# A two-layer diffusion backbone: logits beside the turns, a reordered router, and the last norm on three engines

## The reference

```
logits = h @ w_router                              # 384 x 8
top_v, top_i = lax.top_k(logits, 2); top_p = softmax(top_v)
gates = sum(one_hot(top_i, 8) * top_p[..., None])
act = silu(einsum('bnd,edf->bnef', h, wg)) * einsum('bnd,edf->bnef', h, wu)
y = einsum('bnef,efd->bnd', act * gates[..., None], wd)      # f = 2816
x = layer_norm(ALPHA * x + gate * y, ln_gain, ln_bias)
```

## Time and profile before

| | before |
|---|---|
| median of 3 runs | 2077.76 us (2075.3 to 2078.76) |
| the profiled execution: time, span | 2079.98 us, 2078.2 us |
| instructions | 22944 |
| TensorE busy | 1790.9 us (86%) |
| VectorE, ScalarE, GpSimd busy | 600.3, 392.2, 55.7 us |
| granted TensorE clock, mean | 0.905 of full |
| read from memory | 397.48 MB |

### The profile page before, as it was taken

One profiled execution on the slowest core, in us unless ns is written; L12 is line 12 of the kernel. 1 busy time (PEld: TensorE's weight loads), 2 busy tenths in 40 slices (PEclk: granted clock), 3 DMA queues, 4 the chain that ended last, 5 costly groups with the idle time before them and its releaser, 6 DMA issues.

```text
span 2078.2 us, 22944 instructions
## 1 busy us (share of the span) xinstructions
PE 1790.9 (86%) x8823; PEld 1008.5 (49%) x8824; DVE 600.3 (29%) x1105; ACT 392.2 (19%) x788; POOL 55.7 (3%) x78
## 2 busy tenths in 40 slices
PE   4998888999987978878899986779997699999982
PEld 1764577888854845665234432223333244444320
DVE  1555564333334735653120010111001020000115
ACT  1333414222213323322010010010001010000100
POOL 1000000000000100001000000000000000000000
PEclk8897889999997988978999996679998799999996
DMA  9244414333342444143986669995565954443490
GB/s 327 82 151 146 162 65 156 121 122 122 122 142 102 161 137 161 61 183 134 374 322 240 228 236 389 395 388 192 198 219 190 390 195 144 152 145 125 154 367 38
DMA packets 198798, 401.95 MB, mean 193 GB/s; under 512 B 10872, under 2 KB 51832, under 8 KB 198688
## 3 DMA queue, kind: packets, MB, share of 16 engines
q1 hardware_dynamic: 195280, 389.06, 52.1%
q0 software_dynamic: 3408, 11.34, 1.6%
HBM read 397.48 MB, written 2.88 MB: 193 GB/s over the span
## 4 chain that ended last, share of the span: by engine, by line
PE 75%; DMA 8%; DVE 7%; SPq 4%; issue 3%; ACT 2%; POOL 0%; ACTq 0%; DVEq 0%
PE ps L1423 24%; PE ps L1722 15%; PE ps L1766 7%; PE ps L1727 5%; PE ps L1733 4%; PE ps L1682 3%; DMA d_ring<-in_w_moe_up 3%; SPq L520 3%; PE ps L1380 3%; PE ps L1773 2%; DMA gu_ring<-in_w_moe_up 2%; DMA qkv<-in_w_moe_up 2%; PE ps L1515 2%; PE ps L1779 2%; PE ps L1493 1%
## 5 line engine op out<-in xcount | busy, mean ns | idle before, releaser
L1340 DVE TENSOR_TENSOR cst<-cst,ps 128x256 f32<-128x256 f32 (+2 forms) x92 | 34.3, 373 | 826.9 <-ACT cst L862 826.9
L1423 PE MATMUL ps<-d_ring_parts,scratch_parts 128*128 128x512 f32 (+1 forms) x444 | 172.8, 389 | 10.1 <-issue 5.0
L1722 PE MATMUL ps<-gu_ring,hT 128*128 128x512 f32 x384 | 172.6, 594 | 0.0
L869 ACT ACTIVATE cst<-ps 128x256 f32<-128x256 f32 (+1 forms) x92 | 31.8, 346 | 586.5 <-PE ps L1749 586.5
L1423 PE MATMUL ps<-gu_ring_parts,scratch_parts 128*128 128x512 f32 (+1 forms) x336 | 129.3, 385 | 0.0
L1423 PE MATMUL ps<-d_ring_parts,hT_parts 128*128 128x512 f32 (+1 forms) x312 | 119.6, 383 | 0.0
L1722 PEld LDWEIGHTS ps<-gu_ring,hT 128*128 128x128 f32 x384 | 70.7, 190 | 83.9 <-issue 83.9
L1423 PE MATMUL ps<-gu_ring_parts,o_parts 128*128 128x512 f32 x264 | 104.4, 395 | 0.0
L1682 PE MATMUL ps<-qkv,small 128*128 128x512 f32 x144 | 75.6, 687 | 32.3 <-issue 32.3
L1733 PE MATMUL ps<-gu_ring,hT 128*32 128x256 f32 x960 | 74.1, 451 | 31.3 <-DMA gu_ring<-in_w_moe_up 31.3
L1423 PEld LDWEIGHTS ps<-d_ring_parts,scratch_parts 128*128 128x128 f32 x444 | 84.7, 191 | 29.7 <-issue 5.8
(11 more groups left out here) (280 smaller groups left out, 2662.1 us busy)
## 6 DMA issues: line engine op xcount, KB each, us to landing
gu_ring<-in_w_ada SPq DMA_DIRECT2D x48, 1024.0 KB, 7.7
gu_ring<-in_w_moe_gate SPq DMA_DIRECT2D x96, 512.0 KB, 8.1
gu_ring<-in_w_moe_up SPq DMA_DIRECT2D x96, 512.0 KB, 9.5
gu_ring<-in_w_moe_down SPq DMA_DIRECT2D x96, 512.0 KB, 8.6
d_ring<-in_w_moe_gate SPq DMA_DIRECT2D x48, 512.0 KB, 11.9
d_ring<-in_w_moe_up SPq DMA_DIRECT2D x48, 512.0 KB, 11.3
d_ring<-in_w_moe_down SPq DMA_DIRECT2D x48, 512.0 KB, 10.6
gu_ring<-in_w_in SPq DMA_DIRECT2D x16, 1024.0 KB, 7.3
```

Source lines behind the costliest of these rows:

```text
L1423: ins = pe.matmul(out, a, w, start=(start and n == 0), stop=(stop and n == 2))
L1722: ins = pe.matmul(ps[:, bank, :].rearrange("p (a f) -> p a f", a=2), hT[:, kc, P * g:P * g + P], wt[:, :, FC * h:FC * h + FC], start=st, s ...
```

## The change

1. **Logits in the turns.** The products of block kc follow the turns of block kc + 2, into banks 0 to 2, one for each tile, instead of one run of products after the last turn.
2. **Order of the rows.** The half rows are turned back as k = 3, 4, 5, then 0, 1, 2; only the first three before the prefix. VectorE takes the rests of the second three after the first pick matrix. It also waits for all turns back before it writes the first pick matrix (which lies in `hT`).
3. **Gather ahead.** The gather begins when the first pick matrix and the first tile's rows of places are there; the products of the other two tiles' rows follow blocks 1 and 3 of it. The banks are exchanged: gather 0 to 3, rows of places 4 to 7. Block 0 takes tile 2 first, and waits before each rest. VectorE's table of turns (`sched`) follows its second copy, the clear comes before the last six copies.
4. **First expert's columns** are copied by ScalarE after block 7, from the first half, while the second half is gathered. The wait for the gather's copies moves into TensorE's first step, before the down products.
5. **The last norm.** In steps 4 to 6 of the last expert (a branch in every body) VectorE folds what is there: `y_acc * gate`, and `ALPHA * x +` that. After the last spread it takes each tile straight from PSUM: gate product, add, statistics. ScalarE normalises (scale and bias per row), GpSimd does the powers, and gain and bias of tile 0; VectorE those of tiles 1 and 2. Each tile is stored by SP's queue as it becomes ready.

```
 # TensorE
+routed = l == 1 and which == 1
 for kc in range(KD):
     ... turns of block kc ...
+    if routed and kc >= 2:
+        logits(kc - 2)
...
+def logits(kc):
+    for i in range(NT):
+        ins = pe.matmul(ps[:, i, 0:NE], hT[:, kc, P * i:P * i + P], w_rt[:, kc, :],
+                        start=(kc == 0), stop=(kc == KD - 1))
...
+for k in HALF_ORDER[:3]:                 # [3, 4, 5, 0, 1, 2]
+    turn_back(k)
 ... prefix ...
+for k in HALF_ORDER[3:]:
+    turn_back(k)
+pe.wait_ge(hTok_lo, 3)
+rows_of(0)
 for hf in range(2):
     pe.wait_ge(pick_ready, hf + 1)
     for kc in range(KD):
         m = KD * hf + kc
...
-        for i in range(NT):
+        for n, i in enumerate((2, 0, 1)):
             for part in (h_hi, h_lo):
+                if m == 0 and part is h_lo:
+                    pe.wait_ge(hTok_lo, (3, 5, 6)[n])
...
+        if m in (1, 3):
+            rows_of(1 + m // 2)
+pe.wait_ge(rows_copied, 4)
 pe.wait_ge(sched_ready, 1)
 # ScalarE
+diag_of(0)
+diag_of(1)
 for m in range(0, 16, 2):
+    if m == 8:
+        act.wait_ge(pick_ready, 2)
+        act.wait_ge(gather_act, 4)
+        act.wait_ge(gather_dve, 4)
+        first_columns(slice(0, P))
     ... copy of block m ...
+    if m == 2:
+        diag_of(2)
+    if m == 4:
+        act.wait_ge(rows_mm, NT)
+        ... four copies to where_rows ...
 # VectorE, in an expert's steps
     if 1 <= k <= 3:
         gates_of(k - 1)
+    if 3 <= k <= 5:
+        with dve.If(t == NE - 1):
+            fold(k - 3)
 # VectorE, after the experts
-add_spread(NE)
-residual(1, 1, ...)
+last_rows(0)       # y_acc = PSUM * gate, after two half tiles of the spread
+variance(0)        # x += y_acc; statistics; variance
+last_rows(1)
+shift_of(0)        # -mean * rstd
+variance(1)
+last_rows(2)
+shift_of(1)
+variance(2)
+gain_and_bias(1)
+shift_of(2)
+gain_and_bias(2)
 # ScalarE, after the experts
+for i in range(NT):
+    act.wait_ge(shift_ready, i + 1)
+    act.activation(x[:, i, :], x[:, i, :], ACT.Identity, bias=shift[:, i:i + 1],
+                   scale=rstd[:, i:i + 1]).then_inc(normed, 1)
 # GpSimd, after its loads
+for i in range(NT):
+    ... wait for variance i, power -1/2 ...
+    if i == 0:
+        pool.wait_ge(normed, 1)
+        pool.tensor_tensor(x[:, 0, :], x[:, 0, :], ln_par_end[0], ALU.mult).then_inc(gained_0, 1)
+pool.wait_ge(gained_0, 1)
+pool.tensor_tensor(x[:, 0, :], x[:, 0, :], ln_par_end[1], ALU.add).then_inc(out_ready[0], 1)
 # SyncE, after the last load
+for i in range(NT):
+    sp.wait_ge(out_ready[i], 1)
+    sp.dma_start(dst, x[:, i, :]).then_inc(y_stored, 16)
```

More of the change, by code:

```diff
@@ L385, in build @@
         spread_added = sem("spread_added")
+        folded = sem("folded")
+        shift_ready = sem("shift_ready")
+        normed = sem("normed")
+        gained_0 = sem("gained_0")
+        y_stored = sem("y_stored")
+        out_ready = [sem(f"out_ready{i}") for i in range(NT)]
         gu_plan = []
@@ L1210, in _, with rows_rest @@
                                    ALU.mult))
-            for k in range(6):
-                dve.wait_ge(hTok_hi, k + 1)
+            def rows_rest(n):
+                k = HALF_ORDER[n]
+                dve.wait_ge(hTok_hi, n + 1)
                 dve.tensor_tensor(h_lo[:, k // 2, 512 * (k % 2):512 * (k % 2) + 512], ps[:, 1 + k, :],
@@ L1216, in _, with gathered @@
                                   ALU.subtract).then_inc(hTok_lo, 1)
+            def gathered(m):
+                dve.wait_ge(gather_mm, m + 1)
+                dve.tensor_copy(hT_all[:, m % KD, HALF_SLOTS * (m // KD):HALF_SLOTS * (m // KD) + HALF_SLOTS],
+                                ps[:, GATHER_BANKS[m % 4], 0:HALF_SLOTS]).then_inc(gather_dve, 1)
+            for n in range(3):
+                rows_rest(n)
             dve.wait_ge(prefix_mm, 1)
@@ L1257, in _ @@
                 dve.wait_ge(pick_ready, hf + 1)
+                if hf == 0:
+                    for n in range(3, 6):
+                        rows_rest(n)
+            gathered(1)
+            gathered(3)
             link(dve.tensor_scalar(groups[:, :], size[:, :], 2.5, None, ALU.is_gt))
@@ L1289, in _ @@
             link(ins)
[L1290 to L1295, removed]
+            dve.memset(hT_all[:, :, SLOTS:SLOTS_PADDED], 0.0).then_inc(slots_cleared, 1)
+            for m in range(5, 16, 2):
+                gathered(m)
+            dve.wait_ge(slots_cleared, 1)
+            dve.wait_ge(gather_dve, 8)
             dve.wait_ge(gather_act, 8)
@@ L1306, in add_spread, with fold @@
                     dve.tensor_tensor(ya, ya, ps[:, k, :], ALU.add).then_inc(spread_added, 1)
+            def fold(i):
+                dve.wait_ge(spread_added, 6 * NE + 1)
+                dve.tensor_tensor(y_acc[:, i, :], y_acc[:, i, :], gate[:, min(i, 1), :], ALU.mult).then_inc(folded, 1)
+                dve.wait_ge(folded, 2 * i + 1)
+                dve.scalar_tensor_tensor(out=x[:, i, :], in0=x[:, i, :], scalar=ALPHA, in1=y_acc[:, i, :],
+                                         op0=ALU.mult, op1=ALU.add).then_inc(folded, 1)
             dve.wait_ge(spread_added, 7)
@@ L1623, in _, with turn_back, rows_of @@
                                 ins.then_inc(chunk_done, 1)
[L1626 to L1637, removed]
+            def turn_back(k):
+                i, hf = divmod(k, 2)
+                for m in range(4):
+                    ins = pe.transpose(ps[:, 1 + k, P * m:P * m + P], hT[:, 4 * hf + m, P * i:P * i + P], ident)
+                ins.then_inc(hTok_mm, 1)
+            def rows_of(i):
+                pe.wait_ge(diag_ready, i + 1)
+                for q in range(4):
+                    ins = pe.matmul(ps[:, ROW_BANKS[q], P * i:P * i + P], cst[:, C_ONES:C_ONES + P], diag[:, q, :],
+                                    start=True, stop=True)
+                ins.then_inc(rows_mm, 1)
+            for k in HALF_ORDER[:3]:
+                turn_back(k)
             pe.wait_ge(chosen_ready, 1)
```

92 lines of the change are left out of this document (63 added, 29 removed).

## The result

The changed kernel takes 2048.45 us (median of 4 runs, 2042.39 to 2051.16) against 2078.26 (2075.3 to 2079.45) for the kernel before: ratio 0.9856, 95% interval 0.9833 to 0.988. I had forecast 2059 with a range of 2052 to 2066. The sign was right, the size was not: 29.8 us were gained where 18.9 were summed. The profiled execution took 2047.34 us, span 2045.5.

What follows compares the result with a forecast made beforehand. TensorE was taken as the bound (86% of the span), except in DMA-bound first-expert loading, the router relay and VectorE's last norm. Gains 8.3 + 8.2 + 2.4 = 18.9 us gave 2059 us, range 2052 to 2066.

Steps and rivals of the forecast that it cites:

- Stores: At the end: two tiles leave earlier and the last half megabyte uses SP's queue; 2.4 us gained (2 to 3.3).
- Logits in the turns: Router: logits interleaved with turns, clock falling at 913.0 us; VectorE's copy starts 4.0 us earlier (1.6 to 6.1).
- the clock holds: Rival, router: turns and products together keep the clock full through logits and prefix; kernel at 2054 us, chance 0.15.
- From the logits to the gather's end: Router: places come sooner and the gather starts ahead of the other rows of places; 3.6 us gained (2.2 to 5.5).
- Into the first expert: Gap between gather and expert 0: TensorE's way into the loop takes 2.9 us instead of 3.59; 0.7 gained (0 to 2.4).
- the rival in small: Rival, expert 0: late VectorE entry delays freeing weight parts, so the router's gain shrinks; up to 2067 us, chance 0.08.
- Weight stream: Experts' weight loads: expert 0 starts 8.3 us earlier, within the 7.6 + 1.7 us that the stream allows.
- The pause near 988 us: Sign, first experts: the DMA pause of about 1.7 us, with the ring full, moves to about 980 us.
- The last norm: At the end: folds hidden in the last expert, work split over three engines; 8.2 us gained (6.5 to 9.4).
- exclude each other: Rival, last norm: GpSimd's long operations hold up VectorE, 1.0 to 3 us more than taken; 2061 us, chance 0.10.
- The rival of the slow product: Rival, last norm: GpSimd's product has a slow path; at 25 us an operation the kernel is at 2095, chance 0.03.

Runs made afterwards that it cites:

- neither filler: Unused extra turns in the kernel before: one behind each logit product, ratio 0.9998; or four behind each column block's three, ratio 0.9971; both together 0.9984.

## Why the prediction was wrong

The range missed by 3.5 us. By the steps of the prediction:

- **Stores: the term that failed most.** I priced issue and landing (2.4 us) and never asked what the 3.8 us between the last landing and the end of the span were; they stood in the trace, and the sum left them where they were. Some 3 of them belong to the store on GpSimd's queue; about 1 us stays with SP's. 6.7 us were gained: 2.7 for the early stores, which is what the term was about, and 4.0 for the queue, which it did not have.
- **Logits in the turns.** The mechanism was right, and two terms were mis-sized: 8.0 us gained instead of 4.0. One is the clock's fall at 913 us, which I took over from the trace before. My own rival "the clock holds" had 6.0 for the logits (7.1 with the prefix) and a chance of 0.15. The fall comes with the waits between the turns, which the change fills; it was an error to treat it as fixed in time. The other 2.0 are the price of a block at the full clock: I took 1.25 us from the lengths of two rows (0.44 and 0.81), it comes every 0.95. A row's length holds the end of its last record, which overlaps the next row. By the rows, the three waits before make 2.4 of the 8.0 us (0.68, 0.68, 1.00), and 48 records at 0.107 us (18 of them from 911.50 to 913.43) instead of 0.214 make 5.1. All seven profiles with the logits in the turns show 7.24 or 7.25 us, all four of the unfilled run 15.26 to 15.36: it is no matter of luck.
- **From the logits to the gather's end.** 3.6 taken, 4.6 measured. The prefix ran at the full clock (1.8 gained to the places instead of 0.6). After the places the gather starts 6.6 us earlier and is 3.8 us longer, 2.8 in all where 3.0 was summed. The prefix's clock is not what made the difference, though: with the logits as one run it ran at half, and from the logits to the gather's end 4.4 us were gained all the same, by a shorter gather.
- **Into the first expert.** 0.7 taken, 2.2 measured: TensorE's way into the loop costs 1.4 us (up to 1.95 in the other profiles), not 2.9; the rows bounded it at 3.5, and the four-us loop tops that I leaned on hold the copies of a result too. Its first step runs at the full clock, 1.7 us shorter, and gives 1.4 of that back to VectorE, which enters late: the rival in small, harmless at this size. My 13.3 us from the gather's end for VectorE were right (13.3 to the first turn), and that is what now bounds this stretch: a shorter way for TensorE alone would gain nothing.
- **Weight stream.** Right: expert 0 starts 14.8 us earlier against the second pair of turns (48.2 after it instead of 62.9), and the experts kept their length within the spread of all profiles. The pause near 988 us, which I expected at about 980, does not appear: from 955 to 1000 us no window of 1 us has a DMA share below 0.81.
- **The last norm.** 8.2 taken, 7.5 measured. GpSimd's product takes 2.34 us, under my 2.5, and holds up the second power by 0.36. The two engines do exclude each other: 2.13 us on one shift, where I took 1.2 in all. The Trainium skill, "SBUF — State Buffer", section "Who interferes with whom", says so; the trace agrees, in both directions. ScalarE's pass with scale and bias takes 1.24 us, not 1.06. The fold hides 5.7 us.
- **The rival of the slow product** fell: 2.34 and 3.08 us an operation, the second with its wait; my estimate of 2.2 from the Trainium skill, "GPSIMD Engine Reference", section "3.1 Elementwise — side-by-side cycle accounting", was near.

What stays open: which activity decides when the clock falls. The runs show that filling the waits moves the fall, and that neither filler holds or restores the full clock to the end of the logits. VectorE's 6.7 us into its first expert are unexplained as well; nothing was tried on them.

## What to carry to other kernels

Account for the span to its very end: what lies behind the last landing is a term too, and the last stores on SP's queue instead of GpSimd's took 4 us off it, for a few lines. A clock level seen beside one pattern of work is not a fact of that moment in the program: if an edit fills the waits ahead of narrow products, price them at the full clock as well, and let that be the forecast if the waits are what went. When work is split between VectorE and GpSimd, keep GpSimd's long operations beside VectorE's one-input ones (the statistics took 1.29 us beside GpSimd's 2.34 us product, as without it), or put them where VectorE waits anyhow.

## What was not expected of the hardware

- A final store from GpSimd's queue leaves 4.2 to 4.4 us between the last byte and the end of the span (2074 to 2078.2; 2046.0 to 2050.4 in the changed kernel with that queue); from SP's queue it is about 1 us (2044.6 to 2045.5 in the changed kernel).
- Twenty-four 8-column products take 10.26 us at the half clock, and the same products with 18 turns among them 7.2 us at the full one; the weight loads are busy all the time in both (10.10 us of 913.00 to 923.10, and 7.10 us of 906.40 to 913.50).
- A one-column operation of VectorE with two inputs takes 2.29 us (0.16 alone) while GpSimd reads 1024 columns, and a one-column power of GpSimd 1.45 us (0.54 alone) while VectorE reads two inputs of 1024.
